# Two changes to the mixing stage of a two-block transformer kernel, and 32 bytes of padding in front of its activation operands

## The reference, cut to what matters

```
h = rms_norm_2(x, norm_mix_g)
cb, cc, cin, q, k, v, f_logit, g_logit = split(h @ w_in)
u = causal_dwconv(cc * cin, conv_mix_w)       # 3 taps along the tokens
y_conv = (cb * u) @ w_out_conv
...
gates = sigmoid(g_logit + b_gate)
x = x + (g_conv * y_conv + g_attn * y_attn) @ w_o
```

## Time and profile before

| | |
|---|---|
| Time of the runs | 1268.63 us median of 3 (1262.93 to 1272.05) |
| The profiled execution | 1256.62 us, span 1254.9 us, mean granted clock 0.997 |
| PE busy | 1225.0 us, 98% of the span |
| DVE, ACT, POOL busy | 991.9, 670.5, 185.8 us |

### The profile page before, as it was taken

The page is one execution under the profiler, slowest core; times in us unless marked ns, Lnnn a source line. Parts: engine busy times, 40 slices in busy tenths (PEclk is TensorE's granted clock), DMA queues, the critical chain, the costliest instruction groups (busy, mean ns, idle before and its releaser), DMA issues. The chain is left out here.

```text
span 1254.9 us, 19172 instructions
## 1 busy us (share of the span) xinstructions
PE 1225.0 (98%) x7804; PEld 1074.5 (86%) x7804; DVE 991.9 (79%) x1196; ACT 670.5 (53%) x837; POOL 185.8 (15%) x168
## 2 busy tenths in 40 slices
PE   6999999999999999999999899999999999999997
PEld 5778677889999999997899899657888999988886
DVE  6788764878778688987999857566678899989886
ACT  6462674374454346567545435363344666656555
POOL 5003010002222111100222112000000222202020
PEclk9999999999999999999999999999999999999999
DMA  5422201259999779664599857301324799958765
GB/s 173 141 68 101 68 1 34 84 137 187 180 206 182 135 215 255 131 115 122 116 213 203 178 95 202 118 1 34 116 87 151 125 213 197 182 155 174 207 115 137
DMA packets 144458, 174.14 MB, mean 139 GB/s; under 512 B 5370, under 2 KB 118250, under 8 KB 144242
## 3 DMA queue, kind: packets, MB, share of 16 engines
q0 software_dynamic: 58288, 71.33, 35.3%
q1 hardware_dynamic: 86066, 101.58, 24.0%
q10 hardware_dynamic: 16, 0.00, 0.0%
HBM read 170.78 MB, written 2.11 MB: 138 GB/s over the span
## 5 line engine op out<-in xcount | busy, mean ns | idle before, releaser
L989 ACT ACTIVATE w_hi<-raw 128x1024 fp32r<-128x1024 f32 (+2 forms) x121 | 156.3, 1294 | 208.7 <-PE psum L2521 145.4
L1543 DVE TENSOR_TENSOR w_lo<-raw,w_hi 128x1024 fp32r<-128x1024 f32 (+2 forms) x121 | 184.6, 1527 | 59.8 <-ACT w_hi L989 59.8
L2515 PE MATMUL psum<-act_hi,w_hi 128*128 128x512 f32 x520 | 207.5, 399 | 4.5 <-DVE act_lo L1552 1.7
L2521 PE MATMUL psum<-act_hi,w_lo 128*128 128x512 f32 x520 | 204.5, 393 | 0.1
L2518 PE MATMUL psum<-act_lo,w_hi 128*128 128x512 f32 x520 | 203.7, 392 | 0.0
L2782 PE MATMUL psum<-s_hi,w_hi 128*128 128x256 f32 x704 | 194.4, 276 | 0.8 <-issue 0.8
L2783 PE MATMUL psum<-s_lo,w_hi 128*128 128x256 f32 x704 | 194.3, 276 | 0.0
L2784 PE MATMUL psum<-s_hi,w_lo 128*128 128x256 f32 x704 | 194.3, 276 | 0.0
L2784 PE MATMUL psum<-act_hi,w_lo 128*128 128x256 f32 x528 | 145.7, 276 | 0.0
L2782 PE MATMUL psum<-act_hi,w_hi 128*128 128x256 f32 x528 | 145.7, 276 | 0.0
L2783 PE MATMUL psum<-act_lo,w_hi 128*128 128x256 f32 x528 | 145.7, 276 | 0.0
(11 more groups left out here) (411 smaller groups left out, 2673.3 us busy)
## 6 DMA issues: line engine op xcount, KB each, us to landing
raw<-in_w_in SPq DMA_DIRECT2D x15, 1024.0 KB, 5.3
xz<-in_w_ffn_in POOLq DMA_DIRECT2D x24, 512.0 KB, 6.4
raw<-in_w_ffn_in SPq DMA_DIRECT2D x22, 512.0 KB, 5.1
xz<-in_w_up POOLq DMA_DIRECT2D x21, 512.0 KB, 5.9
raw<-in_w_up SPq DMA_DIRECT2D x18, 512.0 KB, 5.0
raw<-in_w_in SPq DMA_DIRECT2D x16, 512.0 KB, 4.9
v<-in_w_in POOLq DMA_DIRECT2D x15, 512.0 KB, 6.3
x_buf<-in_w_ffn_out POOLq DMA_DIRECT2D x6, 1024.0 KB, 10.3
```

Source lines behind the costliest of these rows:

```text
L989: A(w_at(w_hi, s, h, n - h), home(s, n)[:, h:n], ACT.Copy).then_inc(w_hi_ready, 1)
L1543: V.tensor_tensor(w_at(w_lo, s, h, n - h), home(s, n)[:, h:n], w_at(w_hi, s, h, n - h).bitcast(F32), ALU.subtract).then_inc(w_lo_ready, 1)
L2515: ins = mm(dst, stationary[0], moving[0], start=first, stop=False)
L2521: return mm(dst, stationary[1], moving[0], start=False, stop=last)
```

## The change

Four edits. One row of eight floats (32 bytes in each partition) is allocated in front of `act_hi`; nobody reads or writes it. For round 3 the copy of p1 goes to row 0 of `tmp`, not row 4, so that the copies of rounds 3 and 4 wait only for the reader two rounds back. SP waits for the reader of row 0 before it loads `out` 1's slab there. DVE makes `z_lo` ahead of the split of `out` 0's slab, not behind it.

```diff
@@ -404,6 +404,7 @@
         gain_both = sb("gain_both", [P, DC])
+        sb("act_pad", [P, 8])
         act_scope = ExitStack()
@@ -789,6 +790,7 @@
                     if (kind, i) == ("p4", MIXES - 2):
+                        sp.wait_ge(z_m1, SEVENS + FIRST_GATE + 1)
                         load_slab(mix_at("out", 1))
@@ -1229,8 +1231,8 @@
                     if i >= 2:
-                        act.wait_ge(z_m1, n - (2 if i == 2 else 1))
-                    A(tmp[:, 0 if i == 1 else 4], psum[:, UP_BANK["p1"]], ACT.Copy).then_inc(z_k1, 1)
+                        act.wait_ge(z_m1, n - (2 if 2 <= i <= 4 else 1))
+                    A(tmp[:, 0 if i in (1, 3) else 4], psum[:, UP_BANK["p1"]], ACT.Copy).then_inc(z_k1, 1)
@@ -2049,7 +2051,7 @@
-                rest, k0, k1 = tmp[:, 5], tmp[:, 2 + i % 2], tmp[:, 0 if i == 1 else 4]
+                rest, k0, k1 = tmp[:, 5], tmp[:, 2 + i % 2], tmp[:, 0 if i in (1, 3) else 4]
@@ -2110,6 +2112,10 @@
                     recombine_mix(kind, i)
+                if (kind, i) == ("p6", FIRST_GATE):
+                    dve.wait_ge(src_ready, src_count(C_Z2 + WC - 1))
+                    for c in range(WC):
+                        split_act(C_Z2 + c, z_hi[:, c], z_lo[:, c], conv_u[:, c])
                 for f in MIX_FREES[e]:
                     split_w(f)
@@ -2134,10 +2140,6 @@
                     gated(0)
-                if (kind, i) == ("p6", FIRST_GATE):
-                    dve.wait_ge(src_ready, src_count(C_Z2 + WC - 1))
-                    for c in range(WC):
-                        split_act(C_Z2 + c, z_hi[:, c], z_lo[:, c], conv_u[:, c])
```

## The result

| | before | after |
|---|---|---|
| median of 4 runs each, us | 1265.78 (1259.22 to 1272.05) | 1289.59 (1289.22 to 1289.97) |
| profiled execution, us | 1256.62 | 1289.22 |
| its span, us | 1254.9 | 1287.5 |

The change makes the kernel slower: ratio 1.0226, 95% interval 1.0194 to 1.0258. That it is slower is clear; whether by more than 2% the interval leaves open. The forecast was 1264.6 us, and its range ended at 1277.

What follows compares the result with a forecast made beforehand. The prediction took PE, busy 1225.0 of 1254.9 us, as the bound. Gains of 2.4 us ahead of `out` 0 and 1.6 from the clock, pad 0, made 1268.6 - 4.0 = 1264.6 us, range 1254 to 1277.

Steps and rivals of the forecast that it cites:

- The 32 bytes: Step on the pad ahead of the activations' operands: shifted starts cost PE 0, with bounds of 18.3 us more and 15.5 less.
- Its upper end: Pad's worst case on PE: 4.4 ns on 1,848 matmuls, half on 4,620 of 256 columns, 18.3 us more, time 1282.9.
- The base: Whole run's starting time: 1268.6 us, the median of the runs shown, 12.0 us above the profiled execution.
- The inference from the steadiness: PE's 229 and 233 ns windows: steady under busy and quiet neighbours, so the 4.4 ns between them is no contention.
- The chance of 0.12 for a cost beyond 1%: Part of the rival that the pad slows PE's reads behind it: 0.24 in all, 0.12 of it for beyond 1%.
- The edit to `k1`: Copy of p1, round 4: removes 0.99 us ahead of p4, worth 0.0 by itself because `out` 0 still waits.
- the 2.4 of the sum: `z_lo` ahead of the split on DVE: `out` 0 starts at 711.78, not 714.19, after a 2.15 us gap; gain 2.41.
- The cover of 0.9 us: On DVE, `z_lo` ends at about 709.5, ahead of the split of `out` 0's slab at 710.46, so costs nothing.
- The clock: PE behind the gap ahead of `out` 0: stays at 1.00, giving back 1.6 us; rival that it falls, chance 0.20.
- "-4.0": Sum for the run: 2.4 us from `out` 0's earlier start plus 1.6 from the clock, with the pad at 0.
- The load into `tmp`: SP's load for `out` 1: issued near 701.7, 12.2 us later, landing at 709.2 with 3.8 us of cover; cost nothing.
- The third rival: Pad speeds PE's reads, from 256 columns' excess over 106.7 ns: up to 15.5 us less, 1249.1 us; chance 0.12.

Runs made afterwards that it cites:

- the maps: Kernels of matmuls alone, the whole computation left out, with operand starts moved in steps of 32 bytes; 256 columns took 113.3 to 120.0 ns.
- e6: The changed kernel with 128 bytes of padding in place of 32; 1274.89 us, ratio 1.0096 to the kernel before.
- e7: The changed kernel without the 32 bytes, with 128 bytes in front of part_hi and part_lo alone; 1258.67 us, ratio 0.9973 to the kernel before.
- e8: The changed kernel without the 32 bytes, with part_hi and part_lo 128 bytes further in the second block alone; 1253.99 us, ratio 0.9954 to the kernel before.

## Why the prediction was wrong

**The step that failed is "The 32 bytes": "I take 0, since all other rows show no effect of place".** The pad moved the distance from 64 to 96 bytes modulo 256, and by the paces that the runs showed that costs 39.6 us. 4,620 matmuls of 256 columns x 6.67 ns are 30.8; 1,848 of 512 with activations moving x 4.4 are 8.1; 654 with weights moving x 1.0 are 0.7, a term that the prediction had nowhere. Off go the gaps and the clock of before, 6.2 us, since both are absent in the changed kernel: 33.4. The profiled spans differ by 32.6.

**Its upper end failed too, in one term.** It took 4.4 ns for 1,848 matmuls, which is exact, and "half of it" for the 4,620 of 256 columns. They lose 6.7 ns each, three times the 2.2 that it gave them, and more than a matmul of 512 columns loses. No row showed 256 columns at a second place, and scaling from 512 was a guess about a mechanism that isn't proportional: at distance 0 the runs have 256 columns slower by 6.7 and 512 faster by 1.8. With the true term the bound would have been 1268.6 - 4.0 + 38.9 = 1303.5. It would have covered the result, but from 13.9 us above it, most of that by the next point.

**The base was too high, and that hid part of the miss.** The sum added to its 1252.6 the 12.0 us by which the median of three runs lay above the profiled one ("I take the same difference"). The changed kernel's median is 0.4 us above its profiled run. By profiled executions the forecast missed by 36.6 us (1289.22 against 1252.6), by medians by 25.0: the 11.6 between them are luck. Later timings put the kernel before at 1259.5 to 1261.7, and with those the forecast would have been some 8 us lower.

**The evidence was read the wrong way.** 229 and 233 ns in the earlier trace rows were steady and differed in roles and in which operand starts where; nothing in the rows spoke for the roles. The text put this beside the earlier trace rows, DVE's 1220 ns at two places, and let DVE's row speak for PE. It did not: in the changed kernel, too, the group by form has DVE at 1220 with everything behind the pad moved (columns as in the earlier trace rows):

```profile
L1545 DVE TENSOR_TENSOR w_lo<-xz,w_hi 128x1024 fp32r<-128x1024 f32 x60 | 73.2, 1220 | 24.3 <-ACT w_hi L991 23.1 <-PE psum L2786 1.1
```

DVE is indifferent to what costs PE 5.9%. The inference from the steadiness, no contention with busy neighbours, was right, and the maps confirm it, but a steady difference was the reason to expect that place counts, not a reason against. The chance of 0.12 for a cost beyond 1% was too low for a resource at 98% with one unexplained difference in its rows.

The Trainium skill's page "SBUF — State Buffer", section "Specifications (TRN2)", gives cachelines of 16 bytes. The prediction worked from this that the pad costs 0. Here the measurement differs and decides: a shift by 32 bytes, two such lines, took 256 columns from 113.3 to 120.0 ns. What fails is the inference; the size of a line no run here tests.

**What held, by the version without the pad.** The edit to `k1` is worth nothing by itself: the gap ahead of p4 goes (0.99 us) and comes up again ahead of `out` 0. There it made 2.60 us where 2.15 was predicted, so the two edits save 0.99 + 3.57 - 2.60 = 2.0 us for the 2.4 of the sum. The cover of 0.9 us between `z_lo` and the split is there, as 1.00. The clock stayed, and gave 7.08 - 5.61 = 1.5 us for 1.6. So "-4.0" came out at -3.4, and what `out` 0 waits for is the split at L1544, as forecast. That run then lost about 1.6 us to the second rhythm in the mixing stage (360 matmuls x 4.45 ns), which no step had. The load into `tmp` is issued at 703.66, with the run some 2 us behind the predicted times there, and nothing waits for it. Two small readings of the prediction are off without consequence: `out` 0 ended at 721.27 before, not 721.4, and 4,620, 1,848 and 654 make 7,122 matmuls, not 7,121.

**The third rival** (the pad speeds PE's reads) is refuted for 96. Of the excess over 106.7 ns that it built on, no distance tried gave back anything: 113.3 is the lowest that 256 columns showed.

## What to carry to other kernels

Where PE sets the time, the start of each moving operand against that of its stationary one is a tuning parameter like any other: moving a buffer, even by a pad that nothing reads, can change the pace of every matmul with operands on both sides of it, by up to 6% here. A shift by a multiple of 256 bytes left 113.3 or 117.8 and 228.9 ns as they were. Read PE's pace (matmuls per stretch without a gap) for each product before and after any change to the order of allocations, and distrust a "same" that mixes a good edit with a shifted buffer. An unexplained, steady difference of pace between two products is the first thing to test, and its size at one width did not give that at another. Where the medians of few runs lie far from the profiled run, time the base again before building a forecast on it.

## What the runs showed of the hardware

- PE's pace depends on the distance of the two operands' starts modulo 256 bytes: 256 columns from 113.3 to 120.0 ns, 512 from 227 to 234.4 in steps of 32 bytes, and up to 240.0 at 68. The best distance isn't the same for both widths (64 or 192 for 256 columns, 0 for 512). Why 256 bytes, and why these paces, no run shows.
- At distances 64 and 192 PE has two rhythms for 256 columns, 113.3 and 117.8 ns, and can hold the slower through a stage or more. In the real kernels it was mostly entered behind stalls of PE of 0.1 to 2.6 us, and at times with the first matmul of a product (e6, e7, e8). The runs at distance 64 spread widely: the version without the pad first had ten runs from 1254.3 to 1257.7 and two at 1266.6 and 1268.1, then twelve from 1254.0 to 1261.6. At distances 96 and 0, where the maps show one rhythm, they lie closer: within 0.8 us (the changed kernel), 2.4 (the pad alone) and 1.3 (192 bytes). Of the six profiled runs whose activations are at distance 64, five show the slower rhythm, worth 1.6 to 11.7 us, and the kernel before doesn't; that it explains the spread of the others is argued from the size and not shown.
- A gap of PE of 3.57 us was followed by a granted clock of 0.52 over 3.5 us (mostly the lower of the two levels, 1.2 GHz); gaps of 2.60 and 1.95 us at the same place left it at 1.00 (2.4 GHz).
